# Gate and up products of a feed-forward block: six of 22 tile pairs by Strassen's identity

## The chip, the cores and the metric

One core of one Trainium2 chip. The metric is the device time of one execution in microseconds (us), and less is better.

## The reference

Two layers (depth 2) over 528 tokens (16 meta tokens ahead of 512), model width 1024, hidden width 2816. A layer is a feed-forward block, a mixer (a gated linear recurrence beside latent attention), and a second feed-forward block, each between two RMS norms. The change touches the feed-forward blocks:

```python
def swiglu(u, w_gate, w_up, w_down):
    return (jax.nn.silu(u @ w_gate) * (u @ w_up)) @ w_down

f = swiglu(rms_norm(h, ffn1_pre_g[l]), ffn1_w_gate[l], ffn1_w_up[l], ffn1_w_down[l])
h = h + 0.5 * rms_norm(f, ffn1_post_g[l])
```

## The kernel before

There are six blocks in a row, numbered b = 0 to 5: 0, 2, 3 and 5 are feed-forward, 1 and 4 mixers. Activations lie features by tokens, 128 features to a chunk, in float32. Every product is made of three matmuls, since an operand is split in a high part (rounded to the type that TensorE takes) and a low part (the rest): high by high, weight high by token low, weight low by token high (`tile`, which records all matmuls at L1588, the line of `mm`). Token operands are `xh` and `xl`, weight parts `whi` and `wlo`.

A feed-forward block walks over 22 pairs m of weight tiles, gate m and up m. A tile is 1024 deep and 128 wide, 8 sub-tiles of 128 by 128. A product (`product`) is 8 sub-tiles by 3 matmuls over the tokens: over 528 tokens in two halves of 264, so 48 matmuls, in blocks 0, 2 and 3; over 512 tokens at once, 24 matmuls, in block 5, where the meta tokens are no longer needed. Each product fills one of four pairs of PSUM banks in turn. It waits for its tile's low part, and before its last sub-tile for the next product's bank pair to be free.

```python
                for k in range(DC):
                    if leads and k == DC - 1:
                        unit_free(u + 1, it)
```

A weight tile n passes four engines. SyncE loads it to `raw`, a ring of four slots (`load`, L601), once the low part of the tile four before it is made; ScalarE rounds it to `whi` (`hi`, L748) once TensorE has used the tile four before it; GpSimd subtracts to get `wlo` in four pieces of 128x256 (`lo`, L683); TensorE uses it. Pair m's tail (`hidden`) is: VectorE scales gate (L1301) and up (L1304) by the token norm, which frees the banks; ScalarE takes silu (L920); VectorE multiplies (L1308); ScalarE rounds to `hidh` (L924); VectorE subtracts to `hidl` (L1311). All queues are in program order, written by hand. After 22 pairs come 16 half tiles of the down product over `hidh` and `hidl`.

A block opens (`opening`) with the first three products side by side, so all three are done at one moment, called the opening's end below; pair 1's up product follows, then pair 2. In block 0 VectorE also computes the recurrence's decay rates behind pair 0 (`decay_rates`, L1156 to L1174).

Of the kernel before, what the change touches and what calls it, by code (L numbers as in the profile page):

```python
# [32 lines left out]
P = 128  # L33
# [84 lines left out]

def build_program(nc, a, out, depth, d_ff):
# [125 lines left out]
    with ExitStack() as ctx:  # L245
# [41 lines left out]
        hidl = sb_at("hidl", arena + FC * CH, [P, FC, T], F32R)  # L287

# [159 lines left out]
        lo_ready = sem("lo_ready")  # L448
        slots_used = sem("slots_used")
# [146 lines left out]
        def _(sp):  # L596
            def load(n, src, adv=0):

                sp.wait_ge(lo_ready, n + 1 + adv)
# [22 lines left out]
            for b in range(NB):  # L622
                l, s0 = b // 3, slot0[b]
                if b % 3 == 1:
# [21 lines left out]
                    with sp.Fori(0, DC // 4) as j:  # L646
                        for m in range(4):
                            load(s0 + S_OUT + m, a["w_out"][l, j * 4 + m], j * 4)
                else:
# [3 lines left out]
                    with sp.Fori(1 if b == 0 else 0, FC // 2) as j:  # L653
                        for m in range(2):
                            load(s0 + 2 * m, a[name + "_gate"][l, j * 2 + m], j * 4)
                            load(s0 + 2 * m + 1, a[name + "_up"][l, j * 2 + m], j * 4)
                    with sp.Fori(0, DC // 2) as j:
                        for m in range(2):
                            for q in range(2):
                                load(s0 + 2 * FC + 2 * m + q, a[name + "_down"][l, j * 2 + m, q], j * 4)  # L660
# [15 lines left out]
        def _(pool):  # L676
            def lo(n, adv=0):

                pool.wait_ge(hi_ready, n + 1 + adv)
# [6 lines left out]

            def lo_run(first, last):

                n = first
                while n < last:  # L690
                    k = n
                    while k < last and tiles[k] == tiles[n] and (k in ARENA) == (n in ARENA):
                        k += 1
                    rounds = (k - n) // RING
                    if rounds > 1 and n not in ARENA:
                        with pool.Fori(0, rounds) as j:
                            for m in range(RING):
                                lo(n + m, j * RING)
                        n += rounds * RING
                    while n < k:  # L700
                        lo(n)
                        n += 1
# [15 lines left out]
            for b in range(NB):  # L718
                if b == 0:
                    pool.wait_ge(lo_ready, lo_made(RING - 2))  # L720
# [3 lines left out]
                lo_run(slot0[b] + RING, slot0[b + 1] if b + 1 < NB else NSLOT)  # L724
# [7 lines left out]
        def _(act):  # L732
# [176 lines left out]
            def ffn(b):  # L909
# [1165 lines left out]
```

## Time and profile before

| | us |
|---|---|
| time, median of 3 runs (2030.22 to 2030.52) | 2030.43 |
| the profiled execution, its own time | 2030.33 |
| its span, first to last instruction | 2028.5 |
| TensorE matmul busy | 2014.0 |
| VectorE busy | 697.2 |
| ScalarE busy | 747.9 |
| GpSimd busy | 997.4 |

The profiled execution's time is 1.8 us over its span, and 0.10 us under the median. TensorE's granted clock was 0.999 of full speed. The chain that ended last is TensorE almost throughout.

### The profile page before, as it was taken

The numbers are of one execution on the slowest core, as the hardware profiler recorded it, in microseconds if no ns is written. First come the engines' busy times: TensorE is split into PE (matmuls) and PEld (weight loads), VectorE is DVE, ScalarE is ACT, GpSimd is POOL, SyncE is SP. The second block draws the span as 40 slices with busy tenths as digits, with TensorE's granted clock in tenths as the row PEclk, the third lists the DMA queues.
The fourth block names the chain that finished last, engine by engine and source line by source line (L and its number), as shares of the span: only waits on it lengthen the run. The fifth ranks groups of instructions, "written<-read, shape, count | busy, mean of one in ns | idle before, by whom it ended". The sixth has DMA issues, their size and how long they took to land.

```text
span 2028.5 us, 37353 instructions
## 1 busy us (share of the span) xinstructions
PE 2014.0 (99%) x15084; PEld 1927.0 (95%) x15084; DVE 697.2 (34%) x1093; ACT 747.9 (37%) x1210; POOL 997.4 (49%) x1257
## 2 busy tenths in 40 slices
PE   9999999999999999999999999999999999999998
PEld 8999999999899999999999999999998998888887
DVE  6222210378546222210062222103885462222102
ACT  5222222455556222232252222223555462232221
POOL 3544454475315544454374444544853155554542
PEclk9999999999999999999999999999999999999999
DMA  4322332222101322232122323321222013323321
GB/s 175 103 85 92 98 111 83 69 94 79 63 32 45 106 89 93 85 125 88 57 94 84 93 87 100 113 84 58 96 84 67 32 53 104 97 92 111 114 72 42
DMA packets 48415, 174.85 MB, mean 86 GB/s; under 512 B 5184, under 2 KB 9408, under 8 KB 48320
## 3 DMA queue, kind: packets, MB, share of 16 engines
q1 hardware_dynamic: 48176, 173.40, 26.1%
q8 instruction: 71, 1.16, 0.2%
q14 instruction: 24, 0.20, 0.0%
q10 hardware_dynamic: 144, 0.10, 0.0%
HBM read 171.38 MB, written 2.10 MB: 86 GB/s over the span
## 4 chain that ended last, share of the span: by engine, by line
PE 98%; DVE 1%; ACT 0%; DMA 0%; issue 0%; SPq 0%; DVEq 0%
PE ps L1588 97%; PE ps L1927 1%; DMA h<-in_x 0%; DVE osb L1535 0%; DVE xl L1545 0%; DVE tail_step L1205 0%; PE ps L1806 0%; ACT xh L778 0%; DVE probT L1503 0%; ACT prob L1061 0%; DVE small L1512 0%; DVE h L1210 0%; ACT tmp L1097 0%; ACT xh L1112 0%; DVE wlo L1239 0%
## 5 line engine op out<-in xcount | busy, mean ns | idle before, releaser
L683 POOL TENSOR_TENSOR wlo<-raw,whi 128x256 fp32r<-128x256 f32 (+2 forms) x1148 | 911.9, 826 | 787.4 <-ACT whi L748 787.4
L1588 PE MATMUL ps<-xh,whi 128*128 128x264 f32 (+2 forms) x3000 | 706.1, 298 | 3.2 <-DVE xl L1244 1.3
L1588 PE MATMUL ps<-xl,whi 128*128 128x264 f32 (+2 forms) x3000 | 703.0, 297 | 0.0
L1588 PE MATMUL ps<-xh,wlo 128*128 128x264 f32 (+2 forms) x3000 | 701.6, 297 | 0.0
L1588 PEld LDWEIGHTS ps<-xh,whi 128*128 128x128 f32 x3000 | 489.1, 188 | 21.0 <-DVE wlo L1239 2.3
L1588 PEld LDWEIGHTS ps<-xl,whi 128*128 128x128 f32 x3000 | 487.8, 188 | 14.8
L1588 PEld LDWEIGHTS ps<-xh,wlo 128*128 128x128 f32 x3000 | 487.5, 188 | 14.0
L748 ACT ACTIVATE whi<-raw 128x1024 fp32r<-128x1024 f32 (+2 forms) x289 | 321.4, 1114 | 152.5 <-PE ps L1588 152.4
L1588 PE MATMUL ps<-hidh,whi 128*128 128x264 f32 (+2 forms) x1276 | 313.6, 296 | 0.0
L1588 PE MATMUL ps<-hidh,wlo 128*128 128x264 f32 (+2 forms) x1276 | 312.3, 295 | 0.0
L1588 PE MATMUL ps<-hidl,whi 128*128 128x264 f32 (+2 forms) x1276 | 312.3, 295 | 0.0
L1588 PEld LDWEIGHTS ps<-hidl,whi 128*128 128x128 f32 x1276 | 214.2, 188 | 6.2
L1588 PEld LDWEIGHTS ps<-hidh,wlo 128*128 128x128 f32 x1276 | 213.8, 188 | 5.9
L1588 PEld LDWEIGHTS ps<-hidh,whi 128*128 128x128 f32 x1276 | 213.2, 188 | 6.1
L924 ACT ACTIVATE hidh<-tmp 128x528 f32 (+3 forms) x88 | 56.6, 643 | 412.7 <-DVE tmp L1308 412.7
L1304 DVE TENSOR_TENSOR tmp<-ps,rs_in 128x528 f32<-128x528 f32 (+1 forms) x88 | 61.9, 703 | 407.4 <-PE ps L1588 407.4
L1283 DVE TENSOR_TENSOR tmp<-tmp,tmp 128x264 f32<-128x264 f32 (+3 forms) x52 | 36.3, 698 | 413.5 <-ACT tmp L811 360.2
L920 ACT ACTIVATE tmp<-tmp 128x528 f32<-128x528 f32 (+1 forms) x88 | 56.6, 643 | 264.9 <-DVE tmp L1301 264.8
L1301 DVE TENSOR_TENSOR tmp<-ps,rs_in 128x528 f32<-128x528 f32 (+1 forms) x88 | 61.9, 704 | 218.7 <-PE ps L1588 203.8
L716 POOL TENSOR_TENSOR tmp<-tmp,tmp 128x264 f32<-128x264 f32 (+1 forms) x55 | 45.8, 833 | 103.1 <-ACT tmp L785 100.4
L1311 DVE TENSOR_TENSOR hidl<-tmp,hidh 128x528 f32 (+3 forms) x88 | 63.7, 723 | 80.9 <-ACT hidh L924 80.9
L683 POOL TENSOR_TENSOR w_mix<-raw,w_mix 128x256 fp32r<-128x256 f32 x32 | 25.5, 829 | 106.5 <-ACT w_mix L748 106.5
(192 smaller groups left out, 1685.9 us busy)
## 6 DMA issues: line engine op xcount, KB each, us to landing
raw<-in_ffn_up SPq DMA_DIRECT2D x88, 512.0 KB, 3.5
raw<-in_ffn_down SPq DMA_DIRECT2D x64, 704.0 KB, 4.1
raw<-in_ffn_gate SPq DMA_DIRECT2D x87, 512.0 KB, 3.5
raw<-in_w_in SPq DMA_DIRECT2D x28, 512.0 KB, 3.5
raw<-in_w_out SPq DMA_DIRECT2D x16, 512.0 KB, 3.5
raw<-in_w_q SPq DMA_DIRECT2D x8, 384.0 KB, 3.3
out_t<-h SPq DMA_DIRECT2D x16, 128.0 KB, 1.7
h<-in_x SPq DMA_DIRECT2D x2, 528.0 KB, 5.1
```

Source lines behind the costliest of these rows:

```text
L683: ins = nc.gpsimd.tensor_tensor(w_lo(n)[:, at], raw[:, r, at], w_hi(n)[:, at].bitcast(F32), ALU.subtract)
L716: nc.gpsimd.tensor_tensor(hs, hs, square_of(k, s, trim), ALU.add)\
L748: nc.scalar.activation(w_hi(n)[:, 0:k], raw[:, r, 0:k], ACT.Copy).then_inc(hi_ready, 1)
L920: nc.scalar.activation(toks(tmp[2], trim), toks(tmp[0], trim), ACT.Silu).then_inc(silu_ready, 1)
L924: nc.scalar.activation(toks(hidh[:, mm, :], trim), toks(tmp[3], trim), ACT.Copy).then_inc(hidh_ready, 1)
L1283: nc.vector.tensor_tensor(acc, acc, part(tmp[m % 2], trim), ALU.add).then_inc(sum_ready, 1)
L1301: nc.vector.tensor_tensor(halves(tmp[0], trim), unit(ug, trim, trim and m > 1), halves(rs_in, trim), ALU.mult).then_inc(psum_free[pair_of( ...
L1304: nc.vector.tensor_tensor(halves(tmp[1], trim), unit(uu, trim, trim and m > 0), halves(rs_in, trim), ALU.mult).then_inc(psum_free[pair_of( ...
L1311: nc.vector.tensor_tensor(toks(hidl[:, mm, :], trim), toks(tmp[3], trim), toks(hidh[:, mm, :], trim).bitcast(F32), ALU.subtract).then_inc( ...
L1588: return nc.tensor.matmul(o, w, x, start=start, stop=stop)
L1927: ins = nc.tensor.transpose(ps[:, c0:c0 + P], prob[e % 4][:, k0:k0 + P], ident)
```

## The change

In six pairs of each feed-forward block (4, 6, 8, 10, 12, 13) gate m and up m are taken as one two by two block product: weights by depth half (4 sub-tiles) and by gate or up, tokens by depth half and token half. Strassen's identity (Winograd's form) makes it of seven block products in place of eight. A block product, called a part below, is 4 sub-tiles by 3 matmuls, 12 matmuls, over half the tokens: 264, or 256 in block 5. In order on TensorE, with the slots of the ring:

- slot "gate": part A (to bank pair z) and part B (to the gate bank pair);
- slot "s13": part C and part D, weights that VectorE sums into the ring, tokens sums T1 and T3; D reuses A's bank and waits for `part_copied`;
- slot "s2up": parts E and F, tokens T2 and T4;
- slot "s4", half size: part G.

So a Strassen pair takes four ring slots (3.5 tiles) of which two are loaded, and three bank pairs. New work: VectorE makes the weight sums in `raw` (`sums`: four instructions of 128x512 a pair) and the low parts of s13, s2up and s4 (`low`), which GpSimd doesn't make; GpSimd makes the gate slot's. VectorE adds the parts up (`strassen_sums`: seven of 128x264 on PSUM). ScalarE copies A out (`part_copy`). Once a block, in pairs 0 to 3, the four token sums are made for four depth chunks: ScalarE scales `h` into `t_in` (`sum_inputs`), VectorE makes 16 sums (`t_sums`), ScalarE rounds them (`sum_hi`), VectorE makes their low parts (`t_low`). They lie where `hidh` and `hidl` of pairs 14 to 21 will be. The loops over pairs are written out in all queues; the mixers are not changed.

```diff
+STRASSEN = (4, 6, 8, 10, 12, 13)
+KH = DC // 2
+T_SUMS = 4
...
+                TILES_OF[b, m] = (n, n + 1, n + 2, n + 3)
+                for i, kind in enumerate(("gate", "s13", "s2up", "s4")):
...
+                tiles += [DC, DC, DC, KH]
...
+        def raw_reusable(eng, n):
+            if n >= RING:
+                wait_lo(eng, n - RING)
+                if KIND.get(n - RING) in ("gate", "s2up"):
+                    eng.wait_ge(w_sums, 3 * STRASSEN_N[n - RING] + 3)
...
+                        load(n[2 if m in STRASSEN else 1], a[name + "_up"][l, m])
...
+                def sum_inputs(k):
...
+                def part_copy(m):
+                    q = STRASSEN_N[TILES_OF[b, m][0]]
+                    act.wait_ge(part_mm, 2 * q + 1)
+                    if q:
+                        act.wait_ge(part_added, 6 * q)
+                    nc.scalar.activation(half(tmp[4], trim, 0), bank(FIRST_U[b, m], trim, 0), ACT.Copy)\
+                        .then_inc(part_copied, 1)
+                sum_inputs(0)
+                for m in range(FC):
+                    n = TILES_OF[b, m]
+                    if m in STRASSEN:
+                        part_copy(m)
+                        for i in range(3):
+                            hi(n[i] + RING)
+                        silu(m)
+                        hi(n[3] + RING)
+                        hid_hi(m)
+                        continue
+                    silu(m)
+                    if m:
+                        hi(n[0] + RING)
+                    if m == 2:
+                        sum_hi(2)
+                        sum_inputs(3)
+                    hid_hi(m)
+                    hi(n[1] + RING)
+                    if m < 2:
+                        sum_hi(m)
+                        sum_inputs(m + 1)
+                    elif m == 2:
+                        sum_hi(3)
...
+                def t_sums(k):
+                    dve.wait_ge(t_in_ready, KH * F + k + 1)
+                    dve.wait_ge(t_lo_ready, KH * F + k)
+                    (a0, nt), (a1, _) = span(trim, 0), span(trim, 1)
+                    b11, b12 = t_in[:, 0, a0:a0 + nt], t_in[:, 0, a1:a1 + nt]
+                    b21, b22 = t_in[:, 1, a0:a0 + nt], t_in[:, 1, a1:a1 + nt]
+                    t1, t2, t3, t4 = [t_sum[:, i, 0:nt] for i in range(T_SUMS)]
+                    chain.link(nc.vector.tensor_tensor(t1, b12, b11, ALU.subtract))
+                    nc.vector.tensor_tensor(t3, b22, b12, ALU.subtract)
+                    chain.link(nc.vector.tensor_tensor(t2, b22, t1, ALU.subtract))
+                    nc.vector.tensor_tensor(t4, b21, t2, ALU.subtract).then_inc(t_sum_ready, 1)
+                def t_low(k):
...
+                def sums(n):
+                    kind = KIND.get(n)
+                    if kind is None or kind == "gate":
+                        return
+                    r, q, c = n % RING, STRASSEN_N[n], KH * P
+                    left, right = slice(0, c), slice(c, 2 * c)
+                    if kind == "s13":
+                        raw_reusable(dve, n)
+                        dve.wait_ge(raw_full[(n - 1) % RING], 16 * LOADED_N[n - 1])
+                        dve.wait_ge(raw_full[(n + 1) % RING], 16 * LOADED_N[n + 1])
+                        gate_w, up_w = raw[:, (n - 1) % RING, :], raw[:, (n + 1) % RING, :]
+                        nc.vector.tensor_tensor(raw[:, r, left], up_w[:, left], up_w[:, right], ALU.add)
+                        ins = nc.vector.tensor_tensor(raw[:, r, right], gate_w[:, left], up_w[:, left], ALU.subtract)
+                    elif kind == "s2up":
+                        dve.wait_ge(w_sums, 3 * q + 1)
+                        ins = nc.vector.tensor_tensor(raw[:, r, left], raw[:, (n - 1) % RING, left],
+                                                      raw[:, (n - 2) % RING, left], ALU.subtract)
+                    else:
+                        raw_reusable(dve, n)
+                        dve.wait_ge(w_sums, 3 * q + 2)
+                        ins = nc.vector.tensor_tensor(raw[:, r, left], raw[:, (n - 3) % RING, right],
+                                                      raw[:, (n - 1) % RING, left], ALU.subtract)
+                    ins.then_inc(w_sums, 1)
+                def low(n):
+                    if n in LO_DVE:
+                        dve.wait_ge(hi_ready, n + 1)
+                        k = tiles[n] * P
+                        nc.vector.tensor_tensor(w_lo(n)[:, 0:k], raw[:, n % RING, 0:k], w_hi(n)[:, 0:k].bitcast(F32),
+                                                ALU.subtract).then_inc(lo_dve, 1)
+                def strassen_sums(m, part):
+                    n, z = TILES_OF[b, m], FIRST_U[b, m]
+                    q = STRASSEN_N[n[0]]
+                    x, y = half(tmp[4], trim, 0), half(tmp[4], trim, 1)
+                    c11, c12 = bank(GATE_U[b, m], trim, 0), bank(GATE_U[b, m], trim, 1)
+                    c21, c22 = bank(UP_U[b, m], trim, 0), bank(UP_U[b, m], trim, 1)
+                    if part == 0:
+                        dve.wait_ge(part_copied, q + 1)
+                        dve.wait_ge(slots_used, slot_used(n[0]))
+                        nc.vector.tensor_tensor(c11, x, c11, ALU.add).then_inc(part_added, 1)
+                    elif part == 1:
+                        dve.wait_ge(part_added, 6 * q + 1)
+                        dve.wait_ge(part_mm, 2 * q + 2)
+                        nc.vector.tensor_tensor(x, x, bank(z, trim, 1), ALU.add).then_inc(part_added, 1)
+                        dve.wait_ge(part_added, 6 * q + 2)
+                        dve.wait_ge(slots_used, slot_used(n[1]))
+                        nc.vector.tensor_tensor(y, x, bank(z, trim, 0), ALU.add).then_inc(psum_free[pair_of(z)], 1)
+                        dve.wait_ge(psum_free[pair_of(z)], read_out(z))
+                        nc.vector.tensor_tensor(x, x, c22, ALU.add).then_inc(part_added, 1)
+                        dve.wait_ge(part_added, 6 * q + 3)
+                        nc.vector.tensor_tensor(c22, y, c22, ALU.add).then_inc(part_added, 1)
+                    elif part == 2:
+                        dve.wait_ge(slots_used, slot_used(n[2]))
+                        nc.vector.tensor_tensor(c21, y, c21, ALU.add).then_inc(part_added, 1)
+                    else:
+                        dve.wait_ge(slots_used, slot_used(n[3]))
+                        nc.vector.tensor_tensor(c12, x, c12, ALU.add).then_inc(part_added, 1)
                 dve.wait_ge(rs_pre, 2 * (b + 1))
-                hidden(0)
-                if b == 0:
-                    decay_rates()
-                hidden(1)
-                with dve.Fori(0, FC // 2 - 1) as j:
-                    hidden(2, j)
-                    hidden(3, j)
+                for m in range(FC):
+                    n = TILES_OF[b, m]
+                    nxt = [i + RING for i in n]
+                    sums(nxt[0])
+                    if m in STRASSEN:
+                        strassen_sums(m, 0)
+                        sums(nxt[1])
+                        low(nxt[0])
+                        sums(nxt[2])
+                        low(nxt[1])
+                        strassen_sums(m, 1)
+                        strassen_sums(m, 2)
+                        low(nxt[2])
+                        strassen_sums(m, 3)
+                        gate(m)
+                        up(m)
+                        sums(nxt[3])
+                        hid(m)
+                        low(nxt[3])
+                        hid_lo(m)
+                        continue
+                    gate(m)
+                    if 1 <= m <= 3:
+                        t_low(m if m == 3 else m - 1)
+                    if m == 2:
+                        t_sums(2)
+                    sums(nxt[1])
+                    low(nxt[0])
+                    up(m)
+                    hid(m)
+                    if m == 2:
+                        t_low(2)
+                        t_sums(3)
+                    low(nxt[1])
+                    hid_lo(m)
+                    if m < 2:
+                        t_sums(m)
+                    if b == m == 0:
+                        decay_rates()
...
+            def strassen(b, m, trim, following):
+                n, z, ug, uu = TILES_OF[b, m], FIRST_U[b, m], GATE_U[b, m], UP_U[b, m]
+                q = STRASSEN_N[n[0]]
+                (a0, nt), (a1, _) = span(trim, 0), span(trim, 1)
+                def part(slot, right, operand, o, lead=None):
+                    for k in range(KH):
+                        if lead is not None and k == KH - 1:
+                            unit_free(lead)
+                        c = ((KH if right else 0) + k) * P
+                        wh, wl = w_hi(slot)[:, c:c + P], w_lo(slot)[:, c:c + P]
+                        xhk, xlk = operand(k)
+                        mm(o, wh, xhk, k == 0, False)
+                        mm(o, wh, xlk, False, False)
+                        ins = mm(o, wl, xhk, False, k == KH - 1)
+                    return ins
+                def tokens(upper, at):
+                    return lambda k: (xh[:, k + upper * KH, at:at + nt], xl[:, k + upper * KH, at:at + nt])
+                def sums(i):
+                    return lambda k: (t_hi[:, k, i, 0:nt], t_lo[:, k, i, 0:nt])
+                slot_in(n[0])
+                part(n[0], False, tokens(0, a0), bank(z, trim, 0), ug).then_inc(part_mm, 1)
+                part(n[0], True, tokens(1, a0), bank(ug, trim, 0), uu).then_inc(slots_used, 1)
+                slot_in(n[1])
+                pe.wait_ge(t_lo_ready, KH * (b // 3 * 2 + b % 3 // 2) + KH)
+                part(n[1], False, sums(0), bank(uu, trim, 1))
+                pe.wait_ge(part_copied, q + 1)
+                part(n[1], True, sums(2), bank(z, trim, 0)).then_inc(slots_used, 1)
+                slot_in(n[2])
+                part(n[2], False, sums(1), bank(z, trim, 1)).then_inc(part_mm, 1)
+                part(n[2], True, sums(3), bank(uu, trim, 0)).then_inc(slots_used, 1)
+                slot_in(n[3])
+                part(n[3], False, tokens(1, a1), bank(ug, trim, 1), following).then_inc(slots_used, 1)
...
```

The order in VectorE's queue, pair 0 of block 0 before (pairs differ only in what hides between them):

```order
L1301 TENSOR_TENSOR tmp_65<-ps,rs_in 128x528 [waits slots_used]
L1304 TENSOR_TENSOR tmp_66<-ps,rs_in 128x528 [waits slots_used]
L1308 TENSOR_TENSOR tmp_68<-tmp_67,tmp_66 128x528 [waits silu_ready,psum_free0]
L1311 TENSOR_TENSOR hidl<-tmp_68,hidh 128x528 [waits hidh_ready]
```

And now from the end of pair 2 through pair 3 of block 0 (tmp_65 to tmp_68 are tmp0 to tmp3; `raw` is written by the weight sums):

```order
L1416 TENSOR_TENSOR hidl<-tmp_68,hidh 128x528 [waits hidh_ready]
L1455 TENSOR_TENSOR raw<-raw 128x512 [waits w_sums]
L1395 TENSOR_TENSOR tmp_65<-ps,rs_in 128x528 [waits slots_used]
L1436 TENSOR_TENSOR t_lo<-t_sum,t_hi 128x1056 [waits t_hi_ready]
L1460 TENSOR_TENSOR raw<-raw 128x512 [waits w_sums,lo_ready]
L1468 TENSOR_TENSOR wlo<-raw,whi 128x1024 [waits hi_ready]
L1403 TENSOR_TENSOR tmp_66<-ps,rs_in 128x528 [waits slots_used]
L1411 TENSOR_TENSOR tmp_68<-tmp_67,tmp_66 128x528 [waits silu_ready,psum_free0]
L1468 TENSOR_TENSOR wlo<-raw,whi 128x512 [waits hi_ready]
L1416 TENSOR_TENSOR hidl<-tmp_68,hidh 128x528 [waits hidh_ready]
```

Where pair 0 before has up (L1304) right behind gate (L1301), three new instructions now stand between pair 3's gate (L1395) and up (L1403): the last token sums' low part, a weight sum and a low part for pair 4. One more weight sum stands ahead of gate, and the low part of s4 ahead of `hidl`.

ScalarE's queue, block 0, from pair 3's silu to the copy of part A of pair 4 (tmp_69 is tmp4):

```order
L970 ACTIVATE tmp_67<-tmp_65 128x528 [waits psum_free3]
L799 ACTIVATE whi<-raw 128x1024 [waits w_sums,slots_used]
L974 ACTIVATE hidh<-tmp_68 128x528 [waits hid_ready]
L799 ACTIVATE whi<-raw 128x512 [waits w_sums,slots_used]
L998 ACTIVATE tmp_69<-ps 128x264 [waits part_mm]
```

The copy, on which part D of pair 4 waits, stands behind the rounding of pair 3's hidden chunk and of s4.

ScalarE's queue, block 0, pair 12 and the copy of part A of pair 13:

```order
L998 ACTIVATE tmp_69<-ps 128x264 [waits part_added,part_mm]
L799 ACTIVATE whi<-raw 128x1024 [waits raw_full0,slots_used]
L799 ACTIVATE whi<-raw 128x1024 [waits w_sums,slots_used] x2
L970 ACTIVATE tmp_67<-tmp_65 128x528 [waits psum_free2]
L799 ACTIVATE whi<-raw 128x512 [waits w_sums,slots_used]
L974 ACTIVATE hidh<-tmp_68 128x528 [waits hid_ready]
L998 ACTIVATE tmp_69<-ps 128x264 [waits part_added,part_mm]
```

Here the two copies (the rows that read `ps`) have pair 12's whole tail between them, down to the rounding of its hidden chunk.

## Rows read from the trace of the kernel before

**Rows 1.** The page: busy time, and the chain that ended last
```profile
PE 2014.0 (99%) x15084; PEld 1927.0 (95%) x15084; DVE 697.2 (34%) x1093; ACT 747.9 (37%) x1210; POOL 997.4 (49%) x1257
...
PE 98%; DVE 1%; ACT 0%; DMA 0%; issue 0%; SPq 0%; DVEq 0%
```

**Rows 2.** Timeline, VectorE, block 0: start us, us, engine line op tiles, idle before
```profile
98.39 0.71 DVE L1301 TENSOR_TENSOR tmp<-ps,rs_in 128x528 f32<-128x528 f32 x1 [2.66 <-PE ps L1588]
104.26 0.71 DVE L1304 TENSOR_TENSOR tmp<-ps,rs_in 128x528 f32<-128x528 f32 x1 [5.17 <-PE ps L1588]
...
121.88 0.71 DVE L1301 TENSOR_TENSOR tmp<-ps,rs_in 128x528 f32<-128x528 f32 x1 [2.66 <-PE ps L1588]
```

**Rows 3.** Timeline, VectorE, block 5 (512 tokens)
```profile
1767.48 0.69 DVE L1301 TENSOR_TENSOR tmp<-ps,rs_in 128x512 f32<-128x512 f32 x1 [2.41 <-PE ps L1588]
...
1789.72 0.69 DVE L1301 TENSOR_TENSOR tmp<-ps,rs_in 128x512 f32<-128x512 f32 x1 [2.40 <-PE ps L1588]
```

**Rows 4.** Timeline, TensorE, 256-wide matmuls one after another; 59 steps between these
```profile
1650.60 0.28 PE L1588 MATMUL ps<-xh,whi 128*128 128x256 f32 x1
...
1657.58 0.28 PE L1588 MATMUL ps<-xh,wlo 128*128 128x256 f32 x1
```

**Rows 5.** Timeline, VectorE, start of block 2
```profile
655.62 0.71 DVE L1301 TENSOR_TENSOR tmp<-ps,rs_in 128x528 f32<-128x528 f32 x1 [4.10 <-ACT rs_in L797]
656.25 0.70 DVE L1304 TENSOR_TENSOR tmp<-ps,rs_in 128x528 f32<-128x528 f32 x1
...
659.08 0.71 DVE L1311 TENSOR_TENSOR hidl<-tmp,hidh 128x528 fp32r<-128x528 f32 x1 [0.71 <-ACT hidh L924]
...
661.43 0.71 DVE L1304 TENSOR_TENSOR tmp<-ps,rs_in 128x528 f32<-128x528 f32 x1 [1.03 <-PE ps L1588]
662.17 1.29 DVE L1308 TENSOR_TENSOR tmp<-tmp,tmp 128x528 f32<-128x528 f32 x1
664.17 1.15 DVE L1311 TENSOR_TENSOR hidl<-tmp,hidh 128x528 fp32r<-128x528 f32 x1 [0.71 <-ACT hidh L924]
```

**Rows 6.** Timeline, ScalarE, start of block 2
```profile
655.61 1.28 ACT L738 ACT_TABLE_LOAD   x1
...
658.40 0.65 ACT L924 ACTIVATE hidh<-tmp 128x528 fp32r<-128x528 f32 x1 [0.84 <-DVE tmp L1308]
```

**Rows 7.** Timeline, GpSimd, start of block 2
```profile
660.07 9.34 POOL L683 TENSOR_TENSOR wlo<-raw,whi 128x256 fp32r<-128x256 f32 x12 [2.62 <-ACT whi L748]
669.72 2.81 POOL L683 TENSOR_TENSOR wlo<-raw,whi 128x256 fp32r<-128x256 f32 x4 [0.31 <-ACT whi L748]
```

**Rows 8.** One line's instructions, VectorE: min/median/max ns
```profile
L1239 DVE TENSOR_TENSOR wlo<-raw,whi x4: 691/956/1225, 5.3 to 11.8; 128x512 fp32r<-128x512 f32 x2, 128x1024 fp32r<-128x1024 f32 x2
...
L1253 DVE TENSOR_TENSOR tmp<-tmp,tmp x11: 420/433/962, 13.0 to 24.2; 128x264 f32<-128x264 f32 x11
...
L1187 DVE TENSOR_TENSOR tmp<-f_ffn,ps x56: 414/418/430, 384.1 to 2013.4; 128x264 f32<-128x264 f32 x48, 128x256 f32<-128x256 f32 x8
```

**Rows 9.** One line's instructions, ScalarE
```profile
L748 ACT ACTIVATE whi<-raw x289: 828/1045/1382, 9.6 to 1988.6; 128x1024 fp32r<-128x1024 f32 x109, 128x1408 fp32r<-128x1408 f32 x32, 128x768 fp32r<-128x768 f32 x4
...
L825 ACT ACTIVATE tmp<-ps x48: 362/384/394, 373.1 to 2019.7; 128x264 f32<-128x264 f32 x28, 128x256 f32<-128x256 f32 x20
```

**Rows 10.** Timeline, VectorE, the decay rates in block 0: first, fourth, and what follows
```profile
32.07 0.17 DVE L1156 TENSOR_SCALAR small<-small 128x8 f32<-128x8 f32 x1
32.72 0.49 DVE L1160 TENSOR_TENSOR small<-small 128x8 f32<-128x8 f32 x1
...
38.80 0.70 DVE L1301 TENSOR_TENSOR tmp<-ps,rs_in 128x528 f32<-128x528 f32 x1
```

**Rows 11.** The page, DMA issues: KB each, median us to landing
```profile
raw<-in_ffn_gate SPq DMA_DIRECT2D x87, 512.0 KB, 3.5
```

**Rows 12.** Windows, TensorE: 47 us of the loop and of unrolled code
```profile
98.40:145.40 47.00, 47.00 (x386) 1.00 0.27 89
310.00:357.00 47.00, 47.00 (x389) 1.00 0.24 82
```

More of the change, by code:

```diff
@@ L141, in build_program @@
         n += 1
-        parts = MIX_UNITS if b % 3 == 1 else dict(gu=2 * FC, out=DC)
+        parts = MIX_UNITS if b % 3 == 1 else dict(gu=2 * FC + len(STRASSEN), out=DC)
         for name, k in parts.items():
@@ L146, in build_program @@
     U[NB, "post"] = n
+    GATE_U, UP_U, FIRST_U = {}, {}, {}
+    for b in range(NB):
+        if b % 3 != 1:
+            n = U[b, "gu"]
+            for m in range(FC):
+                FIRST_U[b, m] = n
+                n += m in STRASSEN
+                GATE_U[b, m], UP_U[b, m] = n, n + 1
+                n += 2
+            FIRST_U[b, FC] = n
     PAIR_OF, NTH = {}, {}
@@ L645, in _ @@
                             sp.dma_start(ropet[0][:, :], a["rope"][0]).then_inc(rope0_in, 16)
-                    with sp.Fori(0, DC // 4) as j:
-                        for m in range(4):
-                            load(s0 + S_OUT + m, a["w_out"][l, j * 4 + m], j * 4)
+                    for m in range(DC):
+                        load(s0 + S_OUT + m, a["w_out"][l, m])
                 else:
@@ L652, in _ @@
                         first_loads()
[L653 to L660, printed above, removed]
+                    for m in range(2 if b == 0 else 0, FC):
+                        n = TILES_OF[b, m]
+                        load(n[0], a[name + "_gate"][l, m])
+                        load(n[2 if m in STRASSEN else 1], a[name + "_up"][l, m])
+                    for m in range(DC):
+                        for q in range(2):
+                            load(DOWN0[b] + 2 * m + q, a[name + "_down"][l, m, q])
             for s in range(2):
@@ L685, in lo @@
                 ins.then_inc(lo_ready, 1)
[L687 to L702, printed above, removed]
             def seam(b):
@@ L723, in _ @@
                     seam(b)
-                lo_run(slot0[b] + RING, slot0[b + 1] if b + 1 < NB else NSLOT)
+                for n in range(slot0[b] + RING, slot0[b + 1] if b + 1 < NB else NSLOT):
+                    if n not in LO_DVE:
+                        lo(n)
             for i, k in enumerate(POOL_TAIL):
@@ new lines, in gate @@
+                def gate(m):
+                    ug = GATE_U[b, m]
+                    if m in STRASSEN:
+                        dve.wait_ge(part_added, 6 * STRASSEN_N[TILES_OF[b, m][0]] + 6)
+                    else:
+                        dve.wait_ge(slots_used, slot_used(TILES_OF[b, m][0]))
+                    nc.vector.tensor_tensor(halves(tmp[0], trim),
+                                            unit(ug, trim, trim and m > 1 and m not in STRASSEN),
+                                            halves(rs_in, trim), ALU.mult).then_inc(psum_free[pair_of(ug)], 1)
```

163 lines of the change are left out of this document (107 added, 56 removed).

## The prediction

> **What bounds the kernel now.** I read the page first: TensorE is busy for 2014.0 us of a span of 2028.5, and the chain that ended last is 98% TensorE [rows 1]. So a matmul removed shortens the kernel, unless another queue makes TensorE wait. Then the timeline of the pairs. In block 0 two pairs take 121.88 - 98.39 = 23.49 us, one 11.75, and VectorE is idle until TensorE releases it (2.66 and 5.17 us before gate and up) [rows 2]. 96 matmuls in 11.75 us are 122.4 ns each. In block 5 a pair takes (1789.72 - 1767.48) / 2 = 11.12 us [rows 3], 48 matmuls of 512 columns at 231.7 ns. A 256-wide one costs (1657.58 - 1650.60) / 59 = 118.3 ns [rows 4]. The chip grants the full 2.4 GHz (1.00) in the loop and in written-out code alike, with 386 and 389 matmuls in 47 us, so writing out the loops costs TensorE nothing [rows 12].
>
> **What is removed.** A Strassen pair is 7 x 12 = 84 matmuls. In blocks 0, 2 and 3 it takes 84 x 0.1224 = 10.28 us in place of 11.75, a gain of 1.47. In block 5 the wide matmuls are lost too: 84 x 0.1183 = 9.94 against 11.12, a gain of 1.18. Over six pairs that is 18 x 1.47 + 6 x 1.18 = 26.4 + 7.1 = **33.5 us**. The Trainium skill (TensorE: Matmul & The Clock Gate, "Back-to-back issue gap") gives N / 2.4 + 2.5 ns for a warm matmul alone, 112.5, 109.2 and 215.8 ns; by it the gain would be 31.4 us. The rows show 9 to 16 ns more for each, and decide.
>
> **What is added, where the pairs run evenly.** VectorE instructions: 128x512 takes 0.69 us, 128x1024 1.22, 128x264 0.43, on PSUM 0.42 [rows 8]. By the line through these 128x1056 (`t_low`) is 1.25, an estimate. A Strassen pair with its ordinary neighbour has four sums (2.8), low parts (1.22 + 1.22 + 0.69 = 3.1), seven additions (3.0) and two tails of four instructions of 0.71 (5.7): 14.6 us in 10.28 + 11.75 = 22.0 us of TensorE. Following the queue, the tail of a Strassen pair ends some 7 us after its part G, its neighbour's gate is read 2 to 3 us late, and s4's low part and the copy of A are made 1 to 2 us before parts G and D want them. I cost this at nothing; its cover is that margin. GpSimd has three tiles of 2.81 us in 22 us instead of four [rows 7]. Loads land 3.5 us after issue [rows 11]; the one that can be late is the up tile of the next Strassen pair, issued when GpSimd is done with the neighbour's gate tile, landing about 1 us after part G. VectorE asks for it 2 us after part G.
>
> **What is added at a block's start** does not hide. Take block 2 and count from the opening's end, 661.43 - 5.87 = 655.56 [rows 5]. Up 1, pair 2 and pair 3 are five products, 29.4 us. Parts A to C of pair 4 bring TensorE to 33.8, where part D needs ScalarE's copy, which stands in its queue behind pair 3's hidden chunk. VectorE's way to that chunk's multiply: 8 gate and up readings 0.63 apart (5.0) [rows 5], 4 multiplies and 3 `hidl` (5.0), 16 token sums (6.6: 0.43 each, 0.08 less where one follows another without a wait, as gate and up do), 4 low parts of them (4.7), 4 weight sums (2.5), 2 low parts (2.4): 26.2 us. It waits for ScalarE where it can do nothing else: silu 0 comes behind a table load of 1.28 [rows 6] and two new scalings of 0.65, each `hidl` behind a rounding of 0.65, `t_low` behind roundings of 128x1056, which at 1.045 for 128x1024 [rows 9] are about 1.07: 4.6 us in my walk. And it shares something with GpSimd. In block 2 a multiply of two SBUF operands took 1.29 us at 662.17 and a subtraction 1.15 at 664.17, where both are 0.71 elsewhere, and 12 pieces of GpSimd took 9.34 us where four take 2.81 [rows 5, 7]: the 1.29 is a wait of 0.58 until the running piece ends, and the next piece then waits for VectorE. Gate and up, with one operand in PSUM, stay at 0.71. The Trainium skill (SBUF — State Buffer, "Who interferes with whom") has the rule: VectorE with two SBUF inputs and GpSimd reading SBUF exclude each other for a whole instruction; by that rule, the trace agrees. Nearly all the new work has two SBUF operands, and GpSimd has 16 pieces (tiles 5 to 8) in this stretch. Without meetings the cost is 0; if each of 16 pieces met one instruction for 0.58 it is 9.3 us. I take about 12 meetings at an average of 0.4, since a meeting starts anywhere in a piece: 4.9.
>
> So pair 3's multiply ends at 26.2 + 4.6 + 4.9 = 35.7, its rounding at 36.4, s4's rounding 0.6 later, the copy (0.38 [rows 9]) at 37.3. TensorE has lost **3.5 us** by part D (0.3 of it at part C, which needs the last token sums).
>
> **Pairs 12 and 13** have no ordinary pair between them. Gate 12 is read after VectorE made s13 and s2up of pair 13 in between, 3.2 us after part G of pair 12; part B of pair 13 asks for that bank pair 2.6 us after it. The copy of 13's A stands in ScalarE's queue behind all of pair 12's tail and comes 6 us after part G, where part D could start at 4.4. By the walk 0.9 and 1.1 us: **2.0 us** a block.
>
> **Block 0** adds the decay rates to VectorE behind pair 0: 6.7 us before [rows 10], of which four instructions held by GpSimd (0.49 and more for 0.17); I take 5.2. Gate 1 is then read at about 13.4, ScalarE rounds tile 6 behind its silu, GpSimd delivers 1.6 us late, pair 4's parts B, C and D wait 2.4, 0.8 and 3.1. With pair 13 that is 10 us. **Block 5** has the same VectorE work in 27.8 us of products: 5.2 at pair 4, 2.0 at pair 13.
>
> Sum given back: 5.5 + 5.5 + 10 + 7.2 = **28.2 us**. Net 33.5 - 28.2 = 5.3 us: 2030.33 - 5.3 = 2025.0 us, on a profiled execution 0.1 under the median, which I leave out. A measurement here can tell 0.2% (4.1 us) from no change.
>
> **Rivals.**
> 1. *The queues keep up.* If GpSimd and VectorE rarely meet, because GpSimd's tiles shift into VectorE's idle moments, only the chains remain: 1.2 us in blocks 2 and 3, 3.6 in block 0, 1.7 in block 5, 7.7 in all; gain 25.8, time 2004.5. For it: pair tails off the start run at 0.71 undisturbed. Against: VectorE is hardly idle in the first 36 us.
> 2. *The port decides, slower than before.* At the block's start nearly every new VectorE instruction waits most of a piece (0.58), and GpSimd, held by each, spreads its 16 pieces over all of the time, so meetings rise to 18 and cost 10.4 us in place of 4.9 in each of four blocks. That gives back 22 more, less what the slack of the first products takes (some 8): 2025 + 14 = 2039. It turns the sign where a block loses over 8.4 us on average. For it: both observed meetings in block 2 cost 0.58 and 0.44.
> 3. *Every pair loses.* The margins of 1 to 2 us in even pairs are used up by meetings or the up tile's load; at 0.5 us for each of 20 such pairs 10 us are lost: 2035.
> 4. *It doesn't do what it says:* half-wide matmuls over token sums run slower than those over tokens. At 2 ns on each of 24 x 84 it costs 4 us: 2029. Against: two shapes and two kinds of operands already run within 1 ns of their line [rows 4, 12].
>
> **Numbers.** Forecast's case, 0.47 (2016 to 2033, of which two thirds lie under 2026.3); rival 1, 0.17; rival 2, 0.23; rival 3 with 4, 0.13. The range: 2009 leaves out half of rival 1, 2040 the worst of rival 2. Faster by over 0.2%: 0.31 + 0.17 + 0.02 = 0.50. Within 0.2%: 0.14 of the forecast's case, 0.04 of rival 2 and 0.07 of rival 3, 0.25. Slower: 0.02 + 0.19 + 0.04 = 0.25.
>
> **What would show it.** Right: an even cycle of 22.0 us from gate to gate two pairs on, in blocks 0, 2 and 3; TensorE idle or stretched at part D of pair 4 in every block (L998's copy ending 37 us after the opening) and at part D of pair 13; VectorE's two-SBUF instructions at 1.0 to 1.3 us in pairs 0 to 3. Block starts of 33 us or less for parts A to C and no wait at D mean rival 1. Pair 4 wrong by more than 3 us, or a cycle over 22.3, make the forecast wrong.

## The result, and the profile after

The changed kernel takes 2039.07 us, median of 5 runs (2037.13 to 2040.78), against 2030.43: 1.0042 times as long, interval 1.0027 to 1.0057. It is **slower by 8.6 us**, where the forecast was 5.3 us faster (2025.0). The profiled execution took 2037.13 us with a span of 2035.3; what follows accounts for the 6.8 us between it and the profiled execution of before (2030.33). The page of after:

```profile
PE 1992.5 (98%) x15084; PEld 1912.8 (94%) x15084; DVE 967.8 (48%) x1509; ACT 834.0 (41%) x1330; POOL 958.1 (47%) x1161
...
PE 85%; DVE 8%; ACT 3%; issue 2%; DMA 1%; POOL 1%; DVEq 0%; SPq 0%; ACTq 0%
```

TensorE's work fell from 2014.0 to 1992.5 us, yet the chain that ended last was 98% TensorE and is 85% now [rows 1]: what was taken from the matmuls came back as waits. (Both pages count 15084 matmuls: blocks 0, 2 and 3 have 3 x 6 x 12 = 216 fewer, and block 5 has 6 x (84 - 48) = 216 more, of half the width.) The pairs of after, VectorE's reading of gate in pairs 6, 8 and 10 of block 0, where TensorE waits for nothing:

```profile
99.97 0.71 DVE L1395 TENSOR_TENSOR tmp<-ps,rs_in 128x528 f32<-128x528 f32 x1
...
121.94 0.71 DVE L1395 TENSOR_TENSOR tmp<-ps,rs_in 128x528 f32<-128x528 f32 x1
...
143.93 0.71 DVE L1395 TENSOR_TENSOR tmp<-ps,rs_in 128x528 f32<-128x528 f32 x1
```

Two pairs take 21.97 and 21.99 us in place of 23.49 [rows 2]: the gain per Strassen pair is the 1.47 us of the forecast, to 0.05. In block 5 two pairs take 1758.16 - 1737.15 = 21.01 us against 22.24 [rows 3]. So the even part went as said, and the loss is elsewhere. Part D of pair 4 in block 2, TensorE, timeline; the number in brackets is the idle time before and what ended it:

```profile
695.38 0.29 PE L1804 MATMUL ps<-t_lo,whi 128*128 128x264 f32 x1
695.51 0.28 PE L1804 MATMUL ps<-t_hi,wlo 128*128 128x264 f32 x1
698.56 0.59 PE L1804 MATMUL ps<-t_hi,whi 128*128 128x264 f32 x1 [2.77 <-ACT tmp L998]
```

What it waited for, VectorE and then ScalarE in the same stretch:

```profile
695.59 0.70 DVE L1403 TENSOR_TENSOR tmp<-ps,rs_in 128x528 f32<-128x528 f32 x1
696.32 0.71 DVE L1411 TENSOR_TENSOR tmp<-tmp,tmp 128x528 f32<-128x528 f32 x1
```

```profile
697.07 0.64 ACT L974 ACTIVATE hidh<-tmp 128x528 fp32r<-128x528 f32 x1 [2.67 <-DVE tmp L1411]
697.61 0.61 ACT L799 ACTIVATE whi<-raw 128x512 fp32r<-128x512 f32 x1
698.13 0.37 ACT L998 ACTIVATE tmp<-ps 128x264 f32<-128x264 f32 x1
```

This is the chain of the prediction: pair 3's multiply, its rounding, s4's rounding, the copy of A. The first gate reading of the block stands at 660.83, so the multiply ends 36.2 us and the copy 37.7 us behind it; the walk had 35.7 and 37.3. What the walk did not have is what TensorE did next. Windows, TensorE; the columns are: stretch, its length, busy us of PE (x matmuls), of PEld, DVE, ACT and POOL, granted clock (1.00 is 2.4 GHz), DMA share, GB/s:

```profile
698.50:705.30 6.80, 6.74 (x32) 6.75 (x33) 2.33 (x6) 2.12 (x3) 5.36 (x8) 0.54 0.46 163
705.30:712.00 6.70, 6.70 (x57) 6.70 (x56) 5.26 (x9) 2.60 (x3) 3.55 (x5) 1.00 0.02 10
...
38.00:45.40 7.40, 7.40 (x63) 7.40 (x62) 6.72 (x27) 2.76 (x4) 0.80 (x2) 1.00 0.00 0
...
49.25:52.65 3.40, 3.40 (x19) 3.40 (x18) 2.83 (x5) 1.36 (x2) 2.60 (x3) 0.52 0.52 154
...
1704.70:1711.50 6.80, 4.40 (x21) 4.10 (x21) 3.54 (x6) 2.86 (x5) 2.21 (x4) 0.51 0.67 231
...
1081.90:1088.70 6.80, 3.23 (x23) 2.62 (x21) 5.54 (x8) 3.11 (x6) 0.00 (x0) 1.00 0.44 145
1088.70:1095.30 6.60, 6.60 (x55) 6.60 (x56) 3.86 (x10) 3.11 (x3) 5.54 (x8) 1.00 0.47 162
```

In block 2 the chip granted 1.2 GHz for 6.8 us, from 697.9, which is 0.7 us before the wait ended, and 32 matmuls ran where 6.7 us later 57 did. The same happened for 3.4 us in block 0, from 1.0 us behind a wait of 2.76 us at pair 3's gate tile, and for 6.8 us in block 5, there from 0.5 us before the wait at part D, behind two shorter ones (1.55 and 0.76 us). In block 3 (the last two rows) the same wait was followed by full speed. In before, once it is up at 4.5 us, the clock falls only at 2025 us, in the last stage.

**The account**, in us. Waits are steps between matmuls beyond their own time, summed; the clock is what the matmuls of the slow stretches took above their own step. The gain is six pairs at 1.47, or 1.18 in block 5. Seen is the time from the reading of gate 0 to that of up 21, after less before.

| block | gain | waits, forecast | waits, seen | clock | sum | seen |
|---|---|---|---|---|---|---|
| 0 | -8.8 | 10 | 12.2 | 0 | +3.4 | +3.7 |
| 2 | -8.8 | 5.5 | 6.3 | 2.8 | +0.3 | +0.5 |
| 3 | -8.8 | 5.5 | 6.4 | 0 | -2.4 | -2.2 |
| 5 | -7.1 | 7.2 | 8.3 | 1.9 | +3.1 | +3.3 |
| all | -33.5 | 28.2 | 33.2 | 4.7 | +4.4 | +5.3 |

In block 0 the slow stretch cost its matmuls 1.6 us, but part B of pair 4 waits for VectorE anyhow: its wait was 1.39 us, and 2.99 and 2.93 in experiments 1 and 2, where no slow stretch came before it. So 2.96, the mean of these two, stands under the waits and 0 under the clock. The other 1.5 of the 6.8 us lie outside the pairs, most of it one wait of TensorE at 519.34 in block 1, of 0.89 us for VectorE's `qt`.

### The profile page after: what moved, and what is told of

Same layout as the page of the kernel before. It is cut to its first block, busy times and chain, and to the rows that moved or that the text cites. A ratio compares the mean times of both kernels' runs of the same rounds, so it can differ in the third digit from the quotient of the medians.

```text
span 2035.3 us, 35735 instructions
## 1 busy us (share of the span) xinstructions
PE 1992.5 (98%) x15084; PEld 1912.8 (94%) x15084; DVE 967.8 (48%) x1509; ACT 834.0 (41%) x1330; POOL 958.1 (47%) x1161
## 4 chain that ended last, share of the span: by engine, by line
PE 85%; DVE 8%; ACT 3%; issue 2%; DMA 1%; POOL 1%; DVEq 0%; SPq 0%; ACTq 0%
PE ps L1804 83%; PE ps L2185 1%; ACT whi L799 1%; DVE wlo L1468 1%; DMA raw<-in_ffn_gate 1%; DVE t_lo L1436 1%; DVE raw L1452 1%; DVE tmp L1411 1%; DVE tmp L1403 1%; POOL wlo L747 1%; DVE t_sum L1429 1%; DVE t_sum L1428 1%; DVE t_sum L1430 0%; ACT t_in L983 0%; DVE raw L1451 0%
## 5 line engine op out<-in xcount | busy, mean ns | idle before, releaser
L1804 PE MATMUL ps<-xh,whi 128*128 128x264 f32 (+2 forms) x2616 | 634.8, 297 | 14.9 <-DVE tmp L1395 7.0
L1804 PE MATMUL ps<-xl,whi 128*128 128x264 f32 (+2 forms) x2616 | 629.6, 295 | 0.0
L1804 PE MATMUL ps<-xh,wlo 128*128 128x264 f32 (+2 forms) x2616 | 628.6, 295 | 0.0
L799 ACT ACTIVATE whi<-raw 128x1024 fp32r<-128x1024 f32 (+3 forms) x337 | 362.8, 1078 | 273.6 <-PE ps L1804 215.6
L1804 PEld LDWEIGHTS ps<-xh,whi 128*128 128x128 f32 x2616 | 436.2, 188 | 31.1 <-DVE tmp L1395 8.7
L1804 PEld LDWEIGHTS ps<-xl,whi 128*128 128x128 f32 x2616 | 435.3, 189 | 10.7
L974 ACT ACTIVATE hidh<-tmp 128x528 fp32r<-128x528 f32 (+1 forms) x88 | 56.3, 640 | 235.5 <-DVE tmp L1411 235.2
L1403 DVE TENSOR_TENSOR tmp<-ps,rs_in 128x528 f32<-128x528 f32 (+1 forms) x88 | 61.5, 699 | 177.4 <-PE ps L1804 177.4
L1804 PE MATMUL ps<-t_hi,whi 128*128 128x264 f32 (+1 forms) x384 | 112.0, 292 | 15.9 <-ACT tmp L998 13.4
L1395 DVE TENSOR_TENSOR tmp<-ps,rs_in 128x528 f32<-128x528 f32 (+1 forms) x88 | 61.7, 701 | 104.1 <-PE ps L1804 88.3
L1804 PE MATMUL ps<-t_lo,whi 128*128 128x264 f32 (+1 forms) x384 | 110.7, 288 | 0.0
L1804 PE MATMUL ps<-t_hi,wlo 128*128 128x264 f32 (+1 forms) x384 | 110.6, 288 | 0.0
```

The costliest lines, as they stand in the source:

```text
L799: nc.scalar.activation(w_hi(n)[:, 0:k], raw[:, r, 0:k], ACT.Copy).then_inc(hi_ready, 1)
L974: nc.scalar.activation(toks(hidh[:, m, :], trim), toks(tmp[3], trim), ACT.Copy).then_inc(hidh_ready, 1)
L1395: nc.vector.tensor_tensor(halves(tmp[0], trim), unit(ug, trim, trim and m > 1 and m not in STRASSEN), halves(rs_in, trim), ALU.mult).then_ ...
L1403: nc.vector.tensor_tensor(halves(tmp[1], trim), unit(uu, trim, trim and m > 0 and m not in STRASSEN), halves(rs_in, trim), ALU.mult).then_ ...
L1804: return nc.tensor.matmul(o, w, x, start=start, stop=stop)
```

## The experiments

Theory A at the start: the waits are about as forecast, and TensorE's clock, which falls behind some of them, is the missing term. Theory B: VectorE and ScalarE are simply later than walked, and the clock costs little.

**1. Keep TensorE busy in the long waits** (`filler`)

```diff
 # tile of a Strassen pair, ahead of part D's wait
+                if m == STRASSEN[0]:
+                    for _ in range(14):
+                        mm(bank(z, trim, 1), w_hi(n[1])[:, 0:P], t_hi[:, 0, 0, 0:nt], True, True)
                 pe.wait_ge(part_copied, q + 1)
 # and ahead of pair 3's gate product in block 0
+                        if b == 0 and m == 3:
+                            for _ in range(14):
+                                mm(bank(GATE_U[b, m], tin, 0), xh[:, 0, 0:P], xh[:, 0, 0:HALF], True, True)
```

> The change as it is, with 14 matmuls of no use ahead of part D's wait at pair 4 in every block, and 14 ahead of pair 3's gate product in block 0 (results are overwritten). They fit in waits of 2.9 and 2.8 us. Theory A (each long wait at pair 4 lets the granted clock fall to 1.2 GHz for 3.4 or 6.8 us, which costs 8.5 us in the profiled run of the change beside the waits themselves): the stretches at 0.5 vanish, pairs 0 to 5 take as long as in block 3 of the change, time 2030 to 2032. Theory B (the waits alone cost, the clock is by the way): the time stays at 2039, or rises by the filler.

Measured: 2032.71 us (10 runs, 2031.94 to 2033.28), ratio to before 1.0011 (1.0001 to 1.002), so **6.4 us faster than after by doing 70 matmuls more**. TensorE at part D of block 2:

```profile
694.00:698.00 4.00, 3.37 (x28) 3.23 (x26) 3.67 (x5) 1.33 (x3) 0.00 (x0) 1.00 0.39 125
698.00:705.00 7.00, 5.94 (x49) 5.77 (x48) 3.72 (x8) 4.25 (x6) 4.79 (x7) 1.00 0.50 183
```

The idle time left at D is 1.2 us, and the clock stays at 1.00 in blocks 2, 3 and 5. Block 2 takes 238.3 us in place of 241.2, block 5 228.9 in place of 231.2, and block 3, which had no slow stretch, 238.4 against 238.6. In block 0 a slow stretch came all the same, from 0.8 us before the end of a wait of 2.99 us at part B that had no filler. That is theory A for blocks 2 and 5, 2.9 and 2.3 us. It isn't the luck of one execution: all ten lie at mean granted clocks of 0.997 or 0.998, the five of after at 0.994 or 0.995. The 8.5 us that the expectation gave the clock was too much, and the time lies 0.7 us above its range. Nor were the waits as forecast: they are 5.0 us over, so theory A is half of the answer.

**2. The copy of A earlier on ScalarE** (`early`)

```diff
 # ScalarE, Strassen pair
-                        part_copy(m)
                         for i in range(3):
                             hi(n[i] + RING)
                         silu(m)
+                        if m + 1 in STRASSEN:
+                            part_copy(m + 1)
                         hi(n[3] + RING)
 # ordinary pair
+                    if m + 1 in STRASSEN:
+                        part_copy(m + 1)
                     hid_hi(m)
```

> The copy of part A is put ahead of the rounding of the previous pair's hidden chunk in ScalarE's queue. Theory A: parts D of pairs 4 and 13 no longer wait (2.9 and 0.8 us a block), some of it comes back as waits of 1.0 us for the next pair's gate tile and 1.1 behind pair 13: 1.9 us a block, 7.8 in all, and the clock stays up in blocks 2, 3 and 5 (6.8 us): 2024 to 2027. Theory B: 7.8 us and no more, 2031.

Measured: 2025.99 us (10 runs, 2025.19 to 2027.91), ratio 0.9978 (0.9969 to 0.9988): **13 us under after, 4.6 us faster than before**. ScalarE starts the copy at 692.36 in block 2, 33.5 us behind gate 0 (658.89), where after has 37.3, and part D waits in no block. TensorE's waits in that stretch:

```profile
690.88 0.39 PE L1807 MATMUL ps<-xh,whi 128*128 128x264 f32 x1 [0.20 <-DVE tmp L1398]
692.14 0.36 PE L1807 MATMUL ps<-t_hi,whi 128*128 128x264 f32 x1 [0.62 <-DVE t_lo L1439]
```

Not all of the 11.5 us of waits at part D of pair 4 and 3.4 at D of pair 13 are won: VectorE's work is as late as it was, so the next pair's gate tile waits 1.4 us in block 2 and 0.9 in block 3, and 0.9 to 2.1 us come up behind pair 13. The blocks take 242.2, 236.8, 236.6 and 229.9, 10.0 us less than in after. The clock still falls in block 0 (68.4 us) and, against the expectation, twice in block 5, for 3.4 us each time. The first of these two has no long wait ahead of it, only 1.55 and 0.76 us at parts B and C: shorter waits than those at D can be enough.

**3. VectorE without GpSimd in its way** (`smallpool`, which leaves out most of the low parts of weight tiles 4 to 8 of each feed-forward block: each piece has 16 columns of 256)

```diff
+                start = any(slot0[b] + RING <= n <= slot0[b] + RING + 4 for b in range(NB) if b % 3 != 1)
-                    at = slice(p * k // LO_PARTS, (p + 1) * k // LO_PARTS)
+                    at = slice(p * k // LO_PARTS, p * k // LO_PARTS + 16 if start else (p + 1) * k // LO_PARTS)
```

> GpSimd's pieces of tiles 4 to 8 of each feed-forward block are cut from 256 to 16 columns; the rest of these tiles' low parts is left out. If what makes VectorE late at a block's start is that it and GpSimd exclude each other (my 4.9 us a block), its new instructions run at 0.43, 0.69 and 1.22 throughout and pair 4's parts B, C and D wait for nothing in blocks 2, 3 and 5, 2.5 us at D in block 0; from gate 0 to the last up 234.5 us in blocks 2 and 3, 224 in block 5; time 2010 to 2014. Rival (VectorE's own work and its waits for ScalarE are too long by themselves): part D still waits 2 us or more in block 2, time over 2025.

Measured: 2014.05 us (one run). The waits at pair 4 are gone in blocks 2 and 3 and are 0.17 us in block 5; in block 0, 2.96 us stay at part D (2.5 expected). Those at pair 13 are as in after (1.10, 0.84). Block 3 takes 234.4 us in place of 238.6: 4.2 us. The first token sums of block 2 in after, then in this kernel, with pair 3's multiply as its last row:

```profile
666.62 0.94 DVE L1429 TENSOR_TENSOR t_sum<-t_in 128x264 f32<-128x264 f32 x1
667.48 0.97 DVE L1430 TENSOR_TENSOR t_sum<-t_in,t_sum 128x264 f32<-128x264 f32 x1
668.48 0.85 DVE L1431 TENSOR_TENSOR t_sum<-t_in,t_sum 128x264 f32<-128x264 f32 x1
669.26 0.69 DVE L1395 TENSOR_TENSOR tmp<-ps,rs_in 128x528 f32<-128x528 f32 x1
```

```profile
661.41 0.43 DVE L1430 TENSOR_TENSOR t_sum<-t_in 128x264 f32<-128x264 f32 x1
661.76 0.45 DVE L1431 TENSOR_TENSOR t_sum<-t_in,t_sum 128x264 f32<-128x264 f32 x1
662.25 0.43 DVE L1432 TENSOR_TENSOR t_sum<-t_in,t_sum 128x264 f32<-128x264 f32 x1
662.60 0.70 DVE L1396 TENSOR_TENSOR tmp<-ps,rs_in 128x528 f32<-128x528 f32 x1
...
685.95 0.71 DVE L1412 TENSOR_TENSOR tmp<-tmp,tmp 128x528 f32<-128x528 f32 x1
```

While four pieces of GpSimd run (3.41 us from 666.53), a sum of 0.43 us takes 0.85 to 0.97, and with GpSimd's pieces at 16 columns it is 0.43 again. The reading of PSUM stays at 0.70 in both. That is the exclusion of [rows 5, 7]. The forecast gave it 4.9 us on the way to pair 3's multiply. Here the multiply ends at 686.66, 31.0 us behind gate 0 (655.62), in place of 36.2: 5.2 us sooner, and the walk without meetings had 26.2 + 4.6 = 30.8. TensorE's time in block 3 falls by 4.2 us only: its waits at pair 4 were 4.1 us in all, and with these gone VectorE is early. Shorter pieces also bring tiles sooner, which no run separates from the meetings.

**4. Pairs that start later and never touch** (`odd5`)

```diff
-STRASSEN = (4, 6, 8, 10, 12, 13)
+STRASSEN = (5, 7, 9, 11, 13)
```

> Strassen pairs 5, 7, 9, 11, 13: one fewer, none adjacent, the first a pair later. The waits at pair 4 and pair 13 should go: left are 0.5 us at part D of pair 5 in blocks 2 and 3, 2.3 in block 5, and in block 0 1.8 for tile 6 and 3.5 at part D. Gain of five pairs 27.9, given back 8.6 and one or two clock falls (up to 5): 2012 to 2019. If instead every Strassen pair lost something (rival 3 of the prediction), it would stay over 2025.

Measured: 2010.86 us, ratio **0.9902** (0.9885 to 0.9919). Blocks 240.4, 233.7, 233.7 and 225.5. Five pairs beat six by 28 us: their gain is 5.6 us smaller, but the waits fall to 5.6 us in block 0 (2.76 at pair 3's gate tile, 2.82 at D), 0.4 in blocks 2 and 3, and 2.1 in block 5. VectorE has 11.75 us more before part D first asks, and each Strassen pair has an ordinary one behind it. The clock falls twice, for 3.4 us in block 0 and in block 5, the second time 1.1 us behind a wait of 2.13 us. The time is 1 us below the expected range.

**5. Only without pair 13** (`no13`: `STRASSEN = (4, 6, 8, 10, 12)`)

> Strassen pairs 4, 6, 8, 10, 12, with pair 13 ordinary, so no two adjacent. If adjacency costs what the trace of the change shows (bank pair 1.09, part D 0.84, the next tile 0.3 to 1.1 us), a block gives up 1.47 us of gain (1.18 in block 5) and wins 2.2 to 3.3: 0.8 us a block, 2.1 in block 5, 4.5 us in all, 2034 to 2036; no wait between 125 and 155 us after gate 0. The waits at pair 4 and the clock falls behind them stay as they are. Rival (the waits come from five Strassen pairs before, as a backlog that grows): the same waits would show at pair 12.

Measured: 2030.70 us (10 runs, 2025.22 to 2033.71), ratio 1.0001 (0.9991 to 1.0011): 4 us better than I expected. Block 3 takes 237.5 us against 238.6, so pair 13 costs 1.1 us a block net (expected 0.8). Of the 4 us, this makes 0.8 over three blocks, and 1.1 are the wait for `qt` in block 1, which is gone (386.9 us, 388.1 in after). What is left, some 2 us, fits the clock. In the profiled execution (2025.22, the lowest) part D waits as in after, and the clock stays:

```profile
696.22 0.39 PE L1804 MATMUL ps<-t_hi,whi 128*128 128x264 f32 x1 [2.77 <-ACT tmp L998]
```

```profile
698.50:705.30 6.80, 6.80 (x58) 6.80 (x57) 4.98 (x10) 2.77 (x3) 6.49 (x10) 1.00 0.31 98
```

58 matmuls in 6.8 us, at 1.00. Over the ten runs the time follows the mean granted clock: 2025.22 and 2027.97 us at 0.997, 2028.20 at 0.996, 2029.07 and 2030.54 at 0.995, 2030.87 to 2032.30 at 0.994, 2033.71 at 0.993. **The same program and, as far as one profile tells, the same waits give 8 us more or less**, by how often the clock falls. A thousandth of mean clock is at most 2 us here, an estimate (it takes 4 us of the span at half speed).

**6. The decay rates behind pair 16 instead of pair 0** (`decay_late`)

```diff
-                    if b == m == 0:
+                    if b == 0 and m == 16:
```

> The decay rates of block 0 are computed behind pair 16, not pair 0; nothing else. The wait of 2.76 us for pair 3's gate tile goes, the one of 1.39 at pair 4's part B falls to 0.34, part D's 2.9 stays: block 0 takes 238.6 us from gate 0 to the last up as block 3, 240.5 to 242 with a clock fall; time 2033 to 2036. Rival (block 0 loses by something else of the program's start, loads or the first tiles): block 0 stays at 243 or more.

Measured: 2032.53 us (10 runs, 2031.21 to 2033.69), ratio 1.0011 (1.0002 to 1.0021). Block 0 takes 240.0 us in place of 244.5, 0.7 less than in before. The wait of 2.76 at pair 3's gate tile is gone and that at part B is 0.37; 2.93 stays at part D, with a slow stretch of 3.4 us from 1.4 us behind it. Both block and time come out 0.5 us under the expected ranges. The wait for `qt` in block 1 stays: from up 21 of block 0 to gate 0 of block 2 it is 388.1 us, as in after, and 386.9 to 387.0 in the kernels with five pairs.

**7 and 8. The best of these together**: `odd5_decay` is 4 with 6, `odd5_decay_early` adds 2.

> Strassen pairs 5, 7, 9, 11, 13 and the decay rates behind pair 16. Block 0 as block 2 of the run with the odd pairs: 233.7 us. Left: 0.4 us at part D of pair 5, 2.1 in block 5. 2010.9 less 6.7: 2003 to 2005.

> The same with the copy of part A ahead of the previous hidden chunk's rounding. Parts D wait for nothing: 0.4 us less in blocks 0, 2, 3 and 2.1 in block 5, where the granted clock no longer falls at pair 5 (1.7): 1999 to 2002.

Measured: 2005.54 us (0.9877, 0.986 to 0.9893), 0.5 above its range, and **2001.40 us (0.9857, 0.984 to 0.9873), 29 us faster than before**. The last one's page:

```profile
PE 1986.6 (99%) x15084; PEld 1909.9 (96%) x15084; DVE 943.1 (47%) x1453; ACT 825.8 (41%) x1318; POOL 971.2 (49%) x1177
...
PE 96%; DVE 2%; ACT 1%; DMA 0%; issue 0%; POOL 0%; SPq 0%; DVEq 0%; ACTq 0%
```

The blocks take 233.1, 233.2, 233.2 and 222.1 us; 240.7 less 5 x 1.47 is 233.4, and 227.9 less 5 x 1.18 is 222.0. So the identity's whole gain arrives, with one wait of 0.28 us left in the four blocks. No clock falls before the end, and four runs lie within 0.23 us. VectorE is busy for 943.1 us, hardly less than the 967.8 of after: it is not how much VectorE has to do, but when it is asked.

## Why the prediction was wrong

- **What is removed: right.** 1.47 us a pair measured 1.5 (two pairs 21.98 for 23.49), and 1.18 measured 1.23. Experiment 8 shows the sum: it saves 29 us with 20 pairs, where 15 x 1.47 + 5 x 1.18 = 28.0.
- **Nothing lost in even pairs: right.** The cycle of 22.0 us came, and between pairs 5 and 12 no step of TensorE is over its own time by more than 0.15 us. Rival 3 is out, and so is rival 4: between gate 4 and up 11 of block 3, matmuls over token sums follow one another after 121.5 ns (mean of 144), those over tokens after 122.4 (mean of 482).
- **Pair 4: right in place and cause, a little low.** The wait at D was 2.93 us (3.2 forecast), at B and C 0.34 and 0.79 where I had 0.3 together: TensorE reaches C 0.6 us before VectorE's last `t_low` is done.
- **Pair 13: low.** Bank 1.09 for 0.9 (1.37 in block 5), D 0.84 for 1.1, and 0.3 to 1.1 at the next tile, which I had not counted: 2.8, 2.2, 2.3 and 3.3 us in blocks 0, 2, 3 and 5 for 2.0 each.
- **Block 0: low.** Pair 3's gate tile ("tile 6") cost 2.76 for 1.6, part B 2.96 for 2.4 (1.39 and the slow stretch before it). Experiment 6 shows that the decay rates were all of the first and most of the second.
- **The step that failed: "Sum given back: 28.2 us".** It was low by two terms. The first had no place in it: the sum prices a wait as idle time alone, with nothing for what a wait does to the clock behind it. The only sentence on the clock said that it is 1.00 in the loop [rows 12], read in a kernel whose TensorE never waits that long; the change makes waits of 2.6 to 2.9 us in every block. In the profiled execution this cost 4.7 us (2.8 in block 2, 1.9 in block 5), and in the median execution probably more: the profiled one is the fastest of the five of after, which lie at mean clocks of 0.995 and 0.994, and the median is 1.9 us above it. The second is size: the waits themselves were 33.2 us, 5.0 over the forecast, 2.2 of it in block 0. With 1.5 us outside the blocks that is 11.2 of the 12.1 us between forecast and profiled time; the last 0.9 us, spread over the four blocks, are not explained. No one of these turned the sign: without the clock's 4.7 us the profiled execution would still be 2.1 us slower than before, and with the waits as forecast 1.8.
- **Rival 1 is out.** It wanted VectorE and GpSimd to meet rarely, and the token sums above meet at once. Experiment 3, which all but takes the meetings away, comes to 2014 us, not 2004.5: its waits are 13.8 us in the four blocks, where the rival had 7.7.
- **Rival 2 had the time, 2039, and the wrong reason.** It wanted VectorE held up 5.5 us more a block than forecast; the multiply it speaks of ended 0.5 us later than in my walk. Experiment 3 puts all that VectorE and GpSimd do to each other at 5.2 us up to that multiply, where the rival had 10.4.

The Trainium skill (TensorE: Matmul & The Clock Gate, "Part 1: The HAM clock gate") says that the array falls to 1.2 GHz when it has been idle, by a monitor that runs freely and is not started by the kernel. By that rule the same wait can cost nothing in one run and some us in the next, and the trace agrees: block 2 against block 3 of after, and the ten runs of `no13`. It could have been read when I forecast, and a rival "the waits at D cost the clock too" would have moved the forecast towards no change; how much such a wait costs, the runs here had to show.

**Open:** why the clock fell in block 2 of after and not in block 3. No run made it fall at will; the falls were only avoided by taking the idle time away. The wait of 0.89 us for `qt` in block 1 is there in every kernel with six pairs that was profiled and in none with five; why stays open. Whether pair 13 would wait with pair 12 ordinary and the rest of the set unchanged stays open too.

## What to carry to other kernels

Where TensorE is 99% busy, price a new wait of it twice: as idle time, and as the slow stretch that may follow, and expect the runs to spread if it does. Before an identity that saves matmuls is judged, look at the first place where the added vector work has a due time: here the same identity, in one pair fewer, placed one pair later and never in two neighbours, turned 8.6 us of loss into 20 us of gain (experiment 4), and with the decay rates and the copy moved out of the way into 29. A copy that frees a bank belongs ahead of a rounding that nobody waits for yet.

## What was not expected of the hardware

- A wait of TensorE of 2.6 to 3.0 us was followed (or overlapped) by 3.4 or 6.8 us at 1.2 GHz in some places and not in others of the same form: yes in blocks 0, 2 and 5 of after, no in block 3 of after and blocks 2, 3 and 5 of `no13`. Shorter waits had it too, at times: 2.13 us in block 5 of `odd5`, 1.55 and 0.76 in block 5 of `early`. A 6.8 us stretch cost 2.8 us of matmuls in block 2, and 1.9 in block 5, where a part of it was idle anyway.
- 14 matmuls (1.7 us) of no use inside a wait of 2.9 us kept the clock and so shortened the kernel: the 1.2 or 1.3 us of idle time left had no slow stretch behind it in blocks 2, 3 and 5.
- A slow stretch on TensorE costs nothing where VectorE is the later one: in block 0 the 1.6 us came off the next wait.
